# RWKV stage: the norm of one pair of heads and the prelude of the next run inside the inversion of the pair between them; r, k and v are mixed by GpSimd while they are projected

## The reference

```
mixed = cur + (prev - cur) * p['rwkv_mu']          # prev: the same rows, one token earlier
r, wd, k, v, ad, gd = _split(mixed, RWKV_SPLIT)
w_log = -jax.nn.softplus(-(p['rwkv_w0'] + jnp.tanh(wd) @ p['rwkv_w2'])) - 0.5
decay = jnp.exp(-jnp.exp(w_log.astype(jnp.float32)))
a = jax.nn.sigmoid(p['rwkv_a0'] + ad @ p['rwkv_a2'])
g = jax.nn.sigmoid(gd) @ p['rwkv_g2']
kk = heads(k * p['rwkv_k_k'])
kk = kk / jnp.maximum(jnp.linalg.norm(kk, axis=-1, keepdims=True), 1e-12)
k = k * (1 + (a - 1) * p['rwkv_k_a'])
...
state = state * w_t + (state . a_t) b_t + v_t k_t ;  y_t = state . r_t     # token by token, a_t = -kk, b_t = kk * a
mean, var = per head over y;  yn = (y - mean) * lax.rsqrt(var + GN_EPS) * ln_w + ln_b
out = (yn + sum(r * k * r_k) * v) * g
```

## Time and profile before

| | us |
|---|---|
| runs | 2694.54, 2681.95, 2690.59 (median 2690.59) |
| profiled execution, span | 2689.2 |
| the same with what lies around it (span + 1.4, the median's distance) | 2690.6 |
| TensorE matmul busy | 2441.0 (91%) |
| VectorE busy | 1407.6 (52%) |
| ScalarE busy | 729.0 (27%) |
| GpSimd busy | 96.0 (4%) |

### The profile page before, as it was taken

How to read it: one execution, slowest core, us unless ns; L and a number is a source line. 1 busy time by engine, 2 the same in 40 slices (tenths; PEclk the granted TensorE clock), 3 DMA queues, 4 the chain that set the end, 5 groups by cost and what they waited for, 6 DMA issues and landing times. The chain is left out here.

```text
span 2689.2 us, 52956 instructions
## 1 busy us (share of the span) xinstructions
PE 2441.0 (91%) x22029; PEld 1832.7 (68%) x22029; DVE 1407.6 (52%) x3005; ACT 729.0 (27%) x1370; POOL 96.0 (4%) x133
## 2 busy tenths in 40 slices
PE   6989999777888978886888988899999999999998
PEld 4566888655556556564555657788888888888886
DVE  3357888861552814714655665756533533443443
ACT  3226888021222312221544551112100100100101
POOL 0020000010100000000111010000000000000000
PEclk8989999987998988987999999999999999999999
DMA  6432232151322312312867756411111111111111
GB/s 175 118 101 82 66 98 71 69 157 34 96 82 69 92 36 85 82 34 84 275 228 265 244 172 205 138 32 47 38 41 48 32 47 44 35 47 32 47 32 75
DMA packets 289132, 252.45 MB, mean 94 GB/s; under 512 B 53575, under 2 KB 240553, under 8 KB 288766
## 3 DMA queue, kind: packets, MB, share of 16 engines
q1 hardware_dynamic: 211382, 198.89, 23.7%
q10 hardware_dynamic: 77512, 50.18, 6.7%
HBM read 200.43 MB, written 48.59 MB: 93 GB/s over the span
## 5 line engine op out<-in xcount | busy, mean ns | idle before, releaser
L1157 PE MATMUL rwkv_banks<-h_chunk,w_gate 128*128 128x384 f32 (+1 forms) x768 | 294.9, 527 | 6.7 <-ACT gate_rows L1500 3.9
L2645 DVE TENSOR_TENSOR x<-x,ps_mm 128x272 f32<-128x272 f32 x280 | 121.5, 438 | 307.5 <-PE ps_mm L2612 307.3
L2636 ACT COPY merged_then_hidden<-ps_mm 128x272 f32<-128x272 f32 x160 | 61.5, 385 | 721.0 <-PE ps_mm L2612 721.0
L2612 PE MATMUL ps_mm<-merged_then_hidden,w_mm 128*128 128x272 f32 x960 | 227.1, 393 | 1.6 <-DVE sums_of_right_sides_ L2865 0.9
L1157 PEld LDWEIGHTS rwkv_banks<-h_chunk,w_gate 128*128 128x128 f32 x768 | 152.8, 211 | 92.4 <-issue 31.0
L2612 PEld LDWEIGHTS ps_mm<-merged_then_hidden,w_mm 128*128 128x128 f32 x960 | 182.2, 190 | 39.9 <-DVE sums_of_right_sides_ L2865 1.3
L2612 PE MATMUL ps_mm<-v_T_and_gates_then_h_mlp,w_mm 128*128 128x272 f32 x864 | 204.5, 392 | 0.0
L2612 PEld LDWEIGHTS ps_mm<-v_T_and_gates_then_h_mlp,w_mm 128*128 128x128 f32 x864 | 164.1, 190 | 33.9
L2612 PE MATMUL ps_mm<-sums_of_right_sides_,w_sums_mm 128*128 128x272 f32 x704 | 165.3, 392 | 0.9 <-DVE sums_of_right_sides_ L2823 0.9
L2645 DVE TENSOR_TENSOR merged_then_hidden<-merged_then_hidden,ps_mm 128x272 f32<-128x272 f32 x120 | 51.7, 436 | 195.2 <-PE ps_mm L2612 195.2
L556 PE MATMUL first_banks<-hT,w_pr 128*128 128x384 f32 (+3 forms) x432 | 150.0, 506 | 3.8 <-PEq L188 3.8
(11 more groups left out here) (474 smaller groups left out, 4226.7 us busy)
## 6 DMA issues: line engine op xcount, KB each, us to landing
k_pages<-in_cache_k SPq DMA_DIRECT2D x128, 256.0 KB, 3.4
v_pages<-in_cache_v SPq DMA_DIRECT2D x128, 256.0 KB, 5.3
w_gate<-in_w_in ACTq DMA_DIRECT2D x48, 512.0 KB, 4.1
w_mm<-in_w_mlp_in SPq DMA_DIRECT2D x32, 512.0 KB, 5.4
w_mm<-in_w_mlp_out SPq DMA_DIRECT2D x32, 512.0 KB, 4.3
w_pr<-in_w_in SPq DMA_DIRECT2D x27, 512.0 KB, 5.2
v_T_and_gates_then_h_mlp<-gates_T SPq DMA_DIRECT2D x16, 544.0 KB, 4.8
gates_T<-gate_rows ACTq DMA_DIRECT2D x32, 192.0 KB, 4.1
```

Of the source, the lines that this page charges most:

```text
L1157: ins = MM(B[:, GB, 0:w], gw[:, n % 2, k, :], hc[:, k, 0:w], start=(k == 0), stop=(k == KO - 1))
L2612: ins = self.nc.tensor.matmul(self.ps[:, c, self.BANK[step], 0:272], left[step][:, k, :], right[step][:, k, 272 * c:272 * c + 272], start= ...
L2636: self.nc.scalar.copy(self.target(step, rows, c), self.out(act, u, step, c)).then_inc(self.by_act, 1)
L2645: self.nc.vector.tensor_tensor(to, to, ps, ALU.add).then_inc(self.by_dve, 1)
```

## The change

In the projection stage GpSimd mixes twelve more blocks, with the same six operations: the four r blocks in `stage_pr` and the four pairs of k and v where they lie. SP stores them, after a wait on `mixed`; r was stored by ScalarE before, k and v by SP after a wait on their writers.

In the RWKV stage the mixed rows are loaded; the differences and mixes of GpSimd and VectorE are gone. A `weave` gives each piece of work a key and writes the instructions of an engine in the order of the keys, with 128 between one pair and the next; the norm of pair i - 1 and the prelude of pair i + 1 get keys inside pair i. The keys only set the order of instructions. All the side matmuls (sums of squares, decay, rate, bonus, mean, variance, output gate) go through one PSUM bank, `FB`, each waiting until the one before has been read (`side`). ScalarE copies three parts out and takes one root over 1088 columns; the reciprocal is done in four parts of 272. Several tiles have two buffers. The gate matmuls go by `slots`: 40 before the first core, 304 in the four rounds together, 40 after the last.

```diff
-                    yield unit_key(u + 1, "P1", 0) + 0.8
-                    sp.wait_ge(S["u_act"], 8 * (u + 1))
-                    sp.wait_ge(S["u_dve"], 6 * (u + 1))
                     rows = (low, gd) if u % 2 == 0 else (stage[:, 0, :], stage[:, 1, :])
                     for n in range(2):
+                        if u < MIXED_PAIRS:
+                            yield unit_key(u + 1, ("P2", "P4")[n], 0)
+                            sp.wait_ge(S["mixed"], 2 + NBK - 5 + 2 * u + n + 1)
+                        else:
+                            yield unit_key(u + 1, "P1", 0) + 0.8 + 0.01 * n
+                            sp.wait_ge(S["u_act"], 8 * (u + 1))
+                            sp.wait_ge(S["u_dve"], 6 * (u + 1))
                         sp.dma_start(p.proj[pair[n][2]], rows[n][:, :]).then_inc(u_out[u % 2], 16)
 
-            weave(once(), weights(), key_pages(), pair_weights(), pair_rows())
+            def r_rows():
+                for n, (_, _, blk) in list(enumerate(blocks))[5:]:
+                    yield 3 * CHUNK * (n + 1) + 9.0
+                    sp.wait_ge(S["mixed"], 2 + n - 4)
+                    sp.dma_start(p.proj[blk], stage[:, (n - 5) % 2, :]).then_inc(stored[(n - 5) % 2], 16)
+
+            weave(once(), weights(), key_pages(), pair_weights(), pair_rows(), r_rows())
...
+
+            def mix(x, mu, n):
                 xs, ds_ = (t[:, TP:NT].rearrange("p (b t) -> p b t", b=NB) for t in (x, dif))
                 ch.mark(G.tensor_tensor(dif[:, 1:TP], x[:, 0:TP - 1], x[:, 1:TP], ALU.subtract))
                 ch.mark(G.tensor_tensor(ds_[:, :, 1:ST], xs[:, :, 0:ST - 1], xs[:, :, 1:ST], ALU.subtract))
                 ch.mark(G.tensor_tensor(ds_[:, :, 0], x[:, NT:NTX], xs[:, :, 0], ALU.subtract))
                 ch.done(G.tensor_scalar(dif[:, 0:1], x[:, 0:1], -1.0, None, ALU.mult))
-                ch.done(G.tensor_scalar(dif[:, :], dif[:, :], mul[:, n:n + 1], None, ALU.mult))
+                ch.done(G.tensor_scalar(dif[:, :], dif[:, :], mu, None, ALU.mult))
                 G.tensor_tensor(x[:, 0:NT], x[:, 0:NT], dif[:, :], ALU.add).then_inc(S["mixed"], 1)
                 pool.wait_ge(S["mixed"], n + 1)
...
+                mix(stage[:, (n - 5) % 2, :], p.vec[:, n - 5, 7:8], 2 + n - 5)
+            for u in range(MIXED_PAIRS):
+                rows = (low, gd) if u % 2 == 0 else (stage[:, 0, :], stage[:, 1, :])
+                for n in range(2):
+                    pool.wait_ge(*emptied(u, "P6" if n == 0 else "P4", 1))
+                    pool.wait_ge(*emptied(u, "P3" if n == 0 else "P7", 1))
+                    c = 2 * (u % 2) + n
+                    mix(rows[n], p.vec[:, c, 8 + u // 2:9 + u // 2], 2 + NBK - 5 + 2 * u + n)
...
 
+def weave(*streams):
+
+    ahead = [[next(s), n, s] for n, s in enumerate(streams)]
+    while ahead:
+        first = min(ahead)
+        try:
+            first[0] = next(first[2])
+        except StopIteration:
+            ahead.remove(first)
...
+    T = 128.0
+    LEVEL, GROUP, SAMPLE = 7.0, 62.0, 98.0
...
+    slots = [(T * -1 + x_, n) for x_, n in ((0, 8), (20.3, 8), (33.1, 8), (47.1, 8), (80, 8))]
+    for i_ in range(HP):
+        slots += [(level_at(i_, l) + x_, n) for l in range(LV) for x_, n in ((3.4, 4), (7.9, 3))]
+        slots += [(T * i_ + 53.5, 3), (T * i_ + 56.5, 8)]
+        slots += [(group_at(i_, g) + x_, 2) for g in range(4) for x_ in (3.0, 7.0)]
+        slots += [(sample_at(i_, step) + 1.5, 2) for step in range(8)]
+    slots += [(T * HP + x_, 8) for x_ in (4.0, 12.0, 22.0, 30.0, 60.0, 70.0, 80.0)]
...
+            emptied = []
+
+            def side(made, kept, left, right):
+
                 for c_, (t0, w) in enumerate(CH):
...
+                    if emptied:
+                        pe.wait_ge(*emptied[-1])
+                    emptied.append((S[kept], len([1 for s, _ in emptied if s is S[kept]]) + 1))
+                    MM(B[:, FB, 0:w], left, right(t0, w), start=True, stop=True).then_inc(S[made], 1)
+                    yield c_
...
+                    yield prelude_at(i, 23.0)
+                    pe.wait_ge(S["act_sq"], i + 1)
+                    for c_ in side("pe_ss", "act_ss", p.halves[:, :], square):
+                        yield prelude_at(i, 26.0 + 3 * c_)
+                    yield prelude_at(i, 33.0)
+                    if i == 0:
+                        pe.wait_ge(S["lora_in"], 16 * 3)
+                    for c_ in side("pe_za", "act_za", w2a2[0:64, cols], lora):
+                        yield prelude_at(i, 36.0 + 3 * c_)
+                    yield prelude_at(i, 42.0)
+                    for c_ in side("pe_zb", "act_zb", w2a2[64:128, cols], rates):
+                        yield prelude_at(i, 45.0 + 3 * c_)
+                    yield prelude_at(i, 112.0)
+                    pe.wait_ge(S["rk_made"], i + 1)
+                    for c_ in side("pe_bon", "bon_done", p.halves[:, :], rk):
+                        yield prelude_at(i, 116.0 + 3 * c_)
...
+                    yield norm_at(i, 3.0)
+                    pe.wait_ge(S["y1_kept"], i * 2 + 2)
+                    pe.wait_ge(S["s_ya"], i + 1)
+                    for c_ in side("gn_mean", "gn_sub", p.halves[:, :], rows_):
+                        yield norm_at(i, 6.0 + 3 * c_)
+                    for c_ in range(3):
+                        yield norm_at(i, 14.0 + 3 * c_)
+                        pe.wait_ge(S["gn_sq"], i * 3 + c_ + 1)
+                        if c_ == 0:
+                            var = side("gn_var", "gn_kept", p.halves[:, :], square)
+                        next(var)
+                    yield norm_at(i, 51.0)
+                    for c_ in side("pe_g", "round_made", g2[:, i * 128:i * 128 + 128], gate_in):
+                        yield norm_at(i, 54.0 + 3 * c_)
...
+            def rounds():
+                for i in range(HP):
+                    for g in range(4):
+                        yield T * i + 0.2 + 1.3 * g
+                        products(i, g)
+                    for l in range(LV):
+                        at_ = level_at(i, l)
+                        for L in range(2):
+                            yield at_ + 1.6 * L
+                            level_p(i, L, l)
+                        yield at_ + 3.2
+                        if l < 2:
+                            turn(i, 2 * l)
+                        elif l < 4:
+                            weigh_values(i, l - 2)
+                        for L in range(2):
+                            yield at_ + 4.6 + 1.6 * L
+                            level_x(i, L, l)
+                        yield at_ + 7.8
+                        if l < 2:
+                            turn(i, 2 * l + 1)
                     for L in range(2):
...
+            weave(rounds(), normalise(), prelude(), gates())
...
+                        yield prelude_at(i, 24.0 + 3 * c_)
+                        act.wait_ge(S["pe_ss"], i * 3 + c_ + 1)
+                        nc.scalar.copy(kn[:, t0:t0 + w], B[:, FB, 0:w]).then_inc(S["act_ss"], 1)
+                    yield prelude_at(i, 32.0)
+                    act.wait_ge(S["act_ss"], i * 3 + 3)
+                    nc.scalar.activation(kn[:, :], kn[:, :], ACT.Sqrt).then_inc(S["act_nrm"], 1)
...
+            def invert_in_place(t, i, at_, sem):
+                for n in range(4):
+                    yield at_ + 2.0 * n
+                    if n == 0:
+                        dve.wait_ge(sem, i + 1)
+                    cols = t[:, 272 * n:272 * n + 272]
+                    ch.mark(V.reciprocal(cols, cols))
...
+                    yield prelude_at(i, 42.5)
+                    dve.wait_ge(S["act_za"], i * 3 + 3)
+                    if i == 0:
+                        dve.wait_ge(S["once_in"], 16 * 3)
...
+                    yield prelude_at(i, 60.0)
+                    dve.wait_ge(S["act_nrm"], i + 1)
+                    ch.done(V.tensor_scalar(kn[:, :], kn[:, :], 1e-12, None, ALU.max))
+                    yield from invert_in_place(kn, i, prelude_at(i, 62.0), S["act_nrm"])
+                    yield prelude_at(i, 71.0)
+                    ch.wait()
+                    ch.done(V.tensor_tensor(kk[:, :], kk[:, :], kn[:, :], ALU.mult))
```

872 lines of the change are left out of this document (438 added, 434 removed).

## The result

The changed kernel took 2728.12 us (median of 4 runs, 2722.72 to 2729.08) against 2688.36 for the kernel before on the same chip: ratio 1.0147, 95% interval 1.0126 to 1.0168. It is slower by 1.5%, where I had forecast 1.8% faster. The profiled execution has a span of 2726.1 us, 36.9 more than before.

What follows compares the result with a forecast made beforehand. TensorE was taken as full except in the four cores (21.9 us idle each), with levels paced by instruction delivery. RWKV stage 21.8 + 113.2 - 144 - 64 + 17 = -56, projection +8: -48 from 2690.6, 2642 us; range 2602 to 2690.

Steps and rivals of the forecast that it cites:

- Step 1: RWKV stage: the three stretches between cores go, 144 us less, their work moving into the rounds.
- Step 2: Rounds: 112 more gates (73.5 us) and 63 side matmuls (39.7 us) add 113 us together.
- Step 3: Rounds: 16 us of added work per round is filled into idle time or clock, 64 us over four rounds.
- B: Rival, rounds: nothing is filled because in-order VectorE and ScalarE put foreign operations ahead of level steps; 2694 us, chance 0.07.
- E: Rival, levels: issue waits are not filled, 10.6 us per core stay, 8 us filled per round; 2674 us, chance 0.12.
- S: Rival, projection stage: a GpSimd mix takes 22 us and paces the pairs; slower, 2712 us, chance 0.06.
- Step 4: Start of the RWKV stage: nothing hides it; scan at 578, first core at 606 us, +21.8 us.
- Step 5: Tail, last core's end to next stage: 41 us instead of 23.7, +17 us, bounds +5 and +25.
- Step 6: Projection stage: twelve more GpSimd mixes slow VectorE by 2.6 us each; +8 us of 0 to 31.

Runs made afterwards that it cites:

- e6: Changed kernel with each level's gates at four places, two each, and four behind the levels instead of eleven: 2692.9 us, ratio 1.0004.
- c1: Changed kernel with gates in four places, own banks for first prelude and last norm, early constants and Exp, 24 tail gates: 2635.6 us, ratio 0.9782.
- e10: Changed kernel with eight gates clumped at one place of each level and four behind the last level instead of eleven: 2759.9 us, ratio 1.0247.
- e13: Changed kernel with only the seven gates of each level in four places (2, 2, 2, 1) instead of two: 2716.4 us, ratio 1.0091.
- e9: Changed kernel with 120 of the 384 gate matmuls left out, 102 of them from the rounds, 18 from the tail: 2712.5 us, ratio 1.0073.
- e7: Changed kernel with each of the 32 quarter reciprocals replaced by a short memset: 2718.5 us, ratio 1.0099.
- e3: Changed kernel with the first pair's decay, rate and squares ahead of the gates and the bonus behind the first products: 2727.1 us, ratio 1.0135.
- e4: Changed kernel with the last pair's mean, variance and root ahead of the remaining gates, five single gates in the gaps: 2719.5 us, ratio 1.0099.
- e1: Changed kernel with the twelve new GpSimd mixes left out, waits and stores kept: 2708.4 us, ratio 1.0076.
- c3: c1 with the old projection stage, VectorE mixing r, k, v inside the rounds, and eight single gates per level in eight places: 2625.7 us, ratio 0.9761.

## Why the prediction was wrong, point by point

Step 1 was right: no stretch between cores is left. Step 2 was near: 108 us of added busy time, some 123 at full clock, against 113.

Step 3 failed, and it is 65 of the 85 us by which the sum (-48) missed the profile's difference (+37). I let 16 us of added work per round stand in idle time or be paid by the clock; it was none (515 + 113 - 630 gives -2 us over four rounds, and 8 us if the added work is taken as 123). By the same sum, with 0.66 us for each gate moved, e6 fills 29 us and c1 56 of the 64 that I had forecast, an estimate; so most of the room was there, and the changed kernel's order did not reach it. The mechanism that I named for the idle time was right: late instruction packets in the levels. The inference from it was wrong. I argued from the mean, 71 us of work against 62 us of delivery, that delivery would no longer limit. But it limits in bursts: seven gates at two places leave the bursts of small matmuls between them as they were, and each still runs into a packet that is 2.2 to 2.9 us under way. The time in which gates run did not bring the packets ahead: 13 of the 15 that ended a wait began 4 to 8.5 us after the one before, though 3.2 are enough. I did write that "a packet can still be late" and priced it at 5 us; they were 9 per round. The second part that I missed is the wait of a gate for the bank of its own block, 5 us per round, which I had not priced at all though the kernel before showed 3.9 us of it. e6 against e10 shows the first, with e13 for a part of it; e6 against e13 shows the second together with the clump and the tail. A third part is only seen in e9: fewer gates lower the clock, and the levels stay 14 to 25 us longer than those of the kernel before, of which the side matmuls are 4 to 10; the rest stays open. The term that I had set against filling (VectorE's operations in the way, 3 us per round) was too large rather than too small: without the reciprocals the rounds win 0.7 us each (e7). Of my signs, the rounds were 149 to 163 us instead of 141, the clock in the levels 0.92, 0.94, 0.94 and 0.87, and the issue waits on the two lines 32.5 us instead of under 20.

Of the rivals, B (nothing filled, 2694) had the size, for the wrong reason: e7 shows that it is not VectorE. E is nearest: 36 of 45 us of issue waits stayed in the changed kernel, but moving the fillers cut them to 19 and 10, so they were fillable. The Trainium skill's word "hidden" ("Runtime: NRT & Kernel Launch", "Instruction fetch mechanics") does not hold here, with 10 to 54 us of waits that end with a packet, by the order of the gates. S, my way to slower, was not it: a mix took 8.2 to 10.3 us, far from 21.

Step 4 was right: +24.0 against +21.8. Its two parts were right as well: the scan started 51.6 us after the projection stage's last matmul (50 forecast), and the first product 28.6 us after the scan (28). A hand-over took 1.4 to 1.8 us behind gates, as estimated, and 2.2 to 2.3 where TensorE stood at the lower clock level. VectorE did not wait for the exponentials here, as it does in e3, where it comes to them earlier.

Step 5 had the right sign and missed 12 us: I took the root in its place of the chain and not in ScalarE's queue, where gate Sigmoids stood ahead of it (e4: -15).

Step 6 was mis-sized: +8 of a range 0 to 31, and it measured 17.5 in the trace (12 to 18 over the runs of equal code) and 20 in e1. VectorE's loss per mix was 2.0 us (I had 2.6), so its 24 us reached the end of the stage almost whole, where I had let three quarters be absorbed. My reading of the earlier trace rows was wrong: I took 6.64 against 4.06 us for a slowing by 1.6. Of these six operations four have their usual length, one takes 1.50 instead of 0.75 us, and the fifth takes 2.97 instead of 0.75 us, until 0.55 us after GpSimd's last operation ended. The Trainium skill ("SBUF — State Buffer", "Who interferes with whom") has the shared port as an exclusive lock for the whole instruction. With that the trace agrees in the 16 operations that ended 0.02 to 0.55 us after one of GpSimd's, and not in the 7 that ended 1.86 us before its end. It was 2.0 us per mix and not up to 8.8 because few operations of VectorE met the lock. They are mostly small ones of the bisection, one after another in a chain, which may be why their loss reached the end of the stage; that is argued.

The filling came out at its written bound of 0, the mixes inside theirs, the tail 4 us beyond its +25: 2642 + 64 + 9 + 12 gives 2727. My range took them as if one at a time could go wrong.

## What to carry to other kernels

Where large matmuls fill gaps between bursts of small ones, count what stands between two fillers and not the mean over the stage: the same 384 gates gave 2693 to 2760 us by their order (e6, e10). Twos between short bursts were enough here, and single ones gave no more (c3). A block that hands its bank over should probably end where other work follows; e6 against e13 shows that only together with two other differences. When work is woven by keys, follow each in-order queue for the first and the last item apart: they have no neighbour to hide in, and cost 53 us here; with own banks and an early root and Exp they cost 8.

## What the hardware showed unexpectedly

- Leaving out 102 large matmuls, some 67 us, made the rounds no shorter; the clock fell from 0.91 to 0.81 and issue waits rose from 36 to 54 us (e9).
- All 70 issue waits over 0.8 us in the rounds of four runs ended 2.2 to 2.9 us after a packet of the instruction queue began, and two packets never began less than 3.2 us apart.
- Twelve GpSimd mixes of 8.2 to 10.3 us each cost VectorE 2.0 us each, and the stage 17 to 20 us, though VectorE was idle for 43 us in it. The 2.0 us are few operations that stand still until GpSimd's has ended, and not all a little slower.
